# Turning and routing raw tokens tile by tile, gathering the first tokens by channel, and loading the exponential's table ahead

## What is computed

```python
    x = x + mixed @ w_out[i]
    x = x + expert_choice_moe(rms_norm(x, norm2_g[i]), w_router[i], w_gate[i], w_up[i], w_down[i])

def expert_choice_moe(h, w_router, w_gate, w_up, w_down):
    cap = EC_CAPACITY * L // N_EXPERTS                    # 64
    aff = jax.nn.softmax(h.astype(F32) @ w_router.astype(F32), axis=-1)
    gate, idx = lax.top_k(aff.transpose(0, 2, 1), cap)
    xs = jax.vmap(lambda hb, ib: hb[ib])(h, idx)
    a = jnp.einsum('becd,edf->becf', xs, w_gate)
    b = jnp.einsum('becd,edf->becf', xs, w_up)
    y = jnp.einsum('becf,efd->becd', jax.nn.silu(a) * b, w_down)
```

## Time and profile before

| what | before |
|---|---|
| time, median of 3 runs | 2307.78 us (2304.1 to 2308.91) |
| time of the profiled execution | 2311.14 us |
| its span, first to last instruction | 2309.3 us |
| PE busy | 2090.5 us (91% of the span) |
| DVE busy / ACT busy | 698.8 us / 539.4 us |
| large DMAs, share of 16 DMA engines | 53.7% |

### The profile page before, as it was taken

One profiled execution on the slowest core, in us unless ns is written; L12 is line 12 of the kernel. 1 busy time (PEld: TensorE's weight loads), 2 busy tenths in 40 slices (PEclk: granted clock), 3 DMA queues, 4 the chain that ended last, 5 costly groups with the idle time before them and its releaser, 6 DMA issues.

```text
span 2309.3 us, 22263 instructions
## 1 busy us (share of the span) xinstructions
PE 2090.5 (91%) x9138; PEld 1263.4 (55%) x9138; DVE 698.8 (30%) x991; ACT 539.4 (23%) x818; POOL 110.1 (5%) x118
## 2 busy tenths in 40 slices
PE   6999959988989898989898978998999889999998
PEld 5766433323333333333333656787777678887866
DVE  4635130010101010101010667622667333224234
ACT  4224111000000000000000553233433233224134
POOL 2420000000000000000000000230000000000000
PEclk9999979999999999999999988999999989999998
DMA  9410617999999999999999221111113202223320
GB/s 232 143 64 2 255 73 325 427 427 428 428 428 429 428 429 429 428 429 428 428 427 386 108 100 55 37 37 37 55 59 132 83 37 109 83 98 128 105 96 37
DMA packets 46116, 512.28 MB, mean 222 GB/s; under 512 B 5585, under 2 KB 5713, under 8 KB 10593
## 3 DMA queue, kind: packets, MB, share of 16 engines
q1 hardware_dynamic: 43616, 504.72, 53.7%
q0 software_dynamic: 2432, 6.61, 1.3%
HBM read 507.08 MB, written 4.19 MB: 221 GB/s over the span
## 4 chain that ended last, share of the span: by engine, by line
PE 68%; DMA 21%; DVE 7%; ACT 3%; issue 1%; SPq 0%; POOL 0%; ACTq 0%; DVEq 0%
DMA arena<-in_w_gu_dram 19%; PE bank L2127 11%; PE bank L2149 5%; PE bank L852 4%; PE bank L853 4%; PE bank L854 4%; PE bank L536 3%; PE bank L537 3%; PE bank L538 3%; PE bank L2095 3%; PE bank L1996 2%; PE bank L877 2%; PE bank L878 2%; PE bank L879 2%; PE bank L2112 2%; PE bank L1856 1%
## 5 line engine op out<-in xcount | busy, mean ns | idle before, releaser
L2127 PE MATMUL bank<-arena 128*64 128x512 f32 x2048 | 483.7, 629 | 82.4 <-DMA arena<-in_w_gu_dram 81.6
L2127 PEld LDWEIGHTS bank<-arena 128*64 128x64 f32 x2048 | 162.9, 144 | 373.4 <-issue 372.3
L2527 DVE TENSOR_TENSOR arena<-arena,bank 128x256 f32<-128x256 f32 x64 | 27.0, 421 | 691.3 <-ACT arena L2730 691.3
L2149 PE MATMUL bank<-arena 128*64 128x512 f32 x1024 | 232.3, 594 | 0.7 <-ACT arena L2734 0.6
L2730 ACT ACTIVATE arena<-bank 128x256 f32<-128x256 f32 x64 | 24.6, 384 | 561.6 <-PE bank L2127 561.6
L2149 PEld LDWEIGHTS bank<-arena 128*64 128x64 f32 x1024 | 76.4, 137 | 141.1 <-issue 141.1
L852 PE MATMUL bank<-input_rounded,weight_rest 128*128 128x512 f32 x352 | 141.3, 401 | 4.9 <-DVE weight_rest L1274 4.9
L853 PE MATMUL bank<-input_rest,weight_rounded 128*128 128x512 f32 x352 | 141.3, 401 | 0.0
L854 PE MATMUL bank<-input_rounded,weight_rounded 128*128 128x512 f32 x352 | 139.1, 395 | 0.0
L536 PE MATMUL bank<-input_rounded,weight_rest 128*128 128x512 f32 x312 | 133.1, 427 | 4.8 <-DVE weight_rest L927 4.8
L537 PE MATMUL bank<-mix_rest,unit_rounded 128*128 128x512 f32 x312 | 127.5, 409 | 0.0
(11 more groups left out here) (455 smaller groups left out, 2946.9 us busy)
## 6 DMA issues: line engine op xcount, KB each, us to landing
arena<-in_w_gu_dram SPq DMA_DIRECT2D x128, 2048.0 KB, 28.8
arena<-in_w_d_dram SPq DMA_DIRECT2D x64, 2048.0 KB, 25.4
arena<-in_wpack_dram SPq DMA_DIRECT2D x83, 1024.0 KB, 4.9
arena<-in_x_dram SPq DMA_DIRECT2D x2, 2048.0 KB, 8.9
arena<-in_xT_dram SPq DMA_DIRECT2D x2, 1024.0 KB, 6.8
x_kept<-arena SPq DMA_DIRECT2D x4, 512.0 KB, 2.6
arena<-x_kept SPq DMA_DIRECT2D x1, 2048.0 KB, 8.2
out_dram<-arena SPq DMA_DIRECT2D x4, 512.0 KB, 2.6
```

What stands on the lines that cost most here:

```text
L2127: last = mm(ab[64 * x:64 * x + 64, :], xsT[:, k, 64 * x:64 * x + 64], w[x][:, k, :], start=k == 0, stop=k == KD - 1)
L2149: last = mm(bank[4 + n][64 * x:64 * x + 64, :], hidT[c % 2][:, P * t + 64 * x:P * t + 64 * x + 64], w[:, x, t, 512 * n:512 * n + 512], sta ...
```

## The change

Five things are changed.

- The raw tokens are turned in halves of a tile (`turn_half(q)`, q from 0 to 7: tile q % 4, channels of half q // 4) into banks 3, 5 and 7 in turn. ACT copies even q, DVE odd q, to `xturn[q]`, with no gain. The halves are placed among the four groups of half 1 of the output products, and so are the router's products, in halves too (`route_half(q)`), except for what can only be done after the last group.
- The gain `norm2` is multiplied once into `wr` by DVE (128x128, ahead of the first addition of half 1).
- ACT takes a dummy exponential of one column right behind its square root, and all four tiles of `h2` are made after the real exponential (before, one ahead of it and three behind).
- In the choice, the first round reads PSUM (the copy to `w16` is gone). `iota` counts from 1 to 64, so the subtraction of one is gone. The first pair's comparison reads the turned ranks in PSUM, ahead of the copy to `rankc`.
- `first_tokens()` replaces `gather(0)` and `turn_tokens(0)`: 32 products with pieces of `h2` stationary and `ohp` moving (128 columns) give the channel-major tokens at once. The copies to `xtok` for the first pair go.

```diff
@@ PE
             for i in range(NT):
                 mixed_product(1, i, range(KD)).then_inc(S("out1_filled"), 1)
-
-            pe.wait_ge(S("out1_added"), nth("out1_added", 8))
-            for k in range(KD):
-                if k >= 2:
-                    pe.wait_ge(S("h2t_a" if k % 2 == 0 else "h2t_v"), k // 2)
-                for i in range(NT):
-                    last = turn(bank[4 + k % 2][:, P * i:P * i + P], x_res[:, i, P * k:P * k + P], ident)
-                last.then_inc(S("h2_turned"), 1)
...
-            for i in range(NT):
-                for k in range(KD):
-                    last = mm(bank[6][:, NE * i:NE * i + NE], hT[:, k, P * i:P * i + P], wr[:, k, :],
-                              start=k == 0, stop=k == KD - 1)
-            last.then_inc(S("lg_filled"), 1)
+                if i == 0:
+                    turn_half(0)
+                    turn_half(1)
+                if i == 1:
+                    for q in (2, 3, 4):
+                        turn_half(q)
+                if i == 2:
+                    turn_half(5)
+                    route_half(0)
+                    route_half(4)
+                if i == 3:
+                    turn_half(6)
+                    route_half(1)
+                    route_half(5)
+            turn_half(7)
+            route_half(2)
+            route_half(6)
+            route_half(3)
+            route_half(7).then_inc(S("lg_filled"), 1)
...
+            def turn_half(q):
+
+                half, i = q // 4, q % 4
+                pe.wait_ge(S("out1_added"), nth("out1_added", max(q + 1, 4)))
+                if q >= 3:
+                    pe.wait_ge(S("h2t_a" if (q - 3) % 2 == 0 else "h2t_v"), (q - 3) // 2 + 1)
+                for k in range(4):
+                    last = turn(turnbank[q % 3][:, P * k:P * k + P], x_res[:, i, P * (4 * half + k):P * (4 * half + k) + P], ident)
+                last.then_inc(S("h2_turned"), 1)
+
+            def route_half(q):
+
+                half, i = q // 4, q % 4
+                pe.wait_ge(S("h2t_a" if q % 2 == 0 else "h2t_v"), q // 2 + 1)
+                if q == 0:
+                    pe.wait_ge(S("wr_made"), 1)
+                for k in range(4):
+                    last = mm(bank[6][:, NE * i:NE * i + NE], xturn[q][:, k, :], wr[:, 4 * half + k, :],
+                              start=q < 4 and k == 0, stop=q >= 4 and k == 3)
+                return last
@@ PE, first pair
+            def first_tokens():
+
+                pe.wait_ge(S("ohp_made"), 2)
+                for n in range(2):
+                    for k in range(4):
+                        for i in range(NT):
+                            last = mm(bank[(3, 7)[n]][:, P * k:P * k + P], h2[:, i, 512 * n + P * k:512 * n + P * k + P],
+                                      ohp[:, i, :], start=i == 0, stop=i == NT - 1)
+                    last.then_inc(S("xs_turned"), 1)
+                pe.sem_inc(S("xs_filled"), 2)
...
-            gather(0)
-            turn_tokens(0)
+            first_tokens()
@@ DVE
                     tt(out=xs, in0=xs, in1=mixbank[c][i][:, :], op=ALU.add).then_inc(S("out1_added"), 1)
+                    if c == 1:
+                        q = 2 * i + 1
+                        dve.wait_ge(S("h2_turned"), nth("h2_turned", q + 1))
+                        dve.tensor_copy(xturn[q], turnbank[q % 3].rearrange("p (k t) -> p k t", t=P)).then_inc(S("h2t_v"), 1)
...
-            own(dve.tensor_copy(w16, bank[7][0:NE, :]))
...
-            ts(rank[0:NE, :], rank[0:NE, :], -1.0, None, ALU.add).then_inc(S("rank_made"), 1)
             dve.wait_ge(S("rank_turned"), nth("rank_turned", 1))
+            for ab in range(2):
+                tt(out=ohp[:, :, CAP * ab:CAP * ab + CAP], in0=iota.unsqueeze(1).to_broadcast([P, NT, CAP]),
+                   in1=l3[:, :, ab:ab + 1].to_broadcast([P, NT, CAP]), op=ALU.is_equal).then_inc(S("ohp_made"), 1)
             own(dve.tensor_copy(rankc, l3))
@@ ACT
+            turned_half(0)
             for i in range(NT):
+                if i:
+                    turned_half(2 * i)
                 act.wait_ge(S("out1_added"), nth("out1_added", 5 + i))
...
             fn(v2, v2, ACT.Sqrt).then_inc(S("n2sd_made"), 1)
...
+            own(fn(stat[:, 344:345], ones[:, 0:1], ACT.Exp))
...
-            fn(h2[:, 0, :], x_res[:, 0, :], ACT.Copy, scale=r2[:, 0:1]).then_inc(S("h2_first"), 1)
...
             fn(lg, lg, ACT.Exp).then_inc(S("lg_exp"), 1)
-            for i in range(1, NT):
+            for i in range(NT):
                 fn(h2[:, i, :], x_res[:, i, :], ACT.Copy, scale=r2[:, i:i + 1]).then_inc(S("h2_made"), 1)
```

More of the change, by code:

```diff
@@ L274, in program @@
         sqd = view(R0 + 8064, D)
+        xturn = [view(R0 + 512 * q, 4, P) for q in range(8)]
+        turnbank = [bank[3], bank[5], bank[7]]
         def unit_slot(u):
@@ L2083, in _ @@
             last.then_inc(S("rank_turned"), 1)
-            pe.wait_ge(S("h2_made"), nth("h2_made", NT - 1))
+            pe.wait_ge(S("h2_made"), nth("h2_made", NT))
             pe.sem_inc(S("hid_turned"), 2)
@@ L2446, in _ @@
             for c in range(N_OUT1 // 2):
+                if c == 1:
+                    dve.wait_ge(S("wr_in"), 32)
+                    n2 = COLS["norm2"]
+                    tt(out=wr, in0=wr, in1=cols[:, n2:n2 + KD].unsqueeze(2).to_broadcast([P, KD, NE]), op=ALU.mult)\
+                        .then_inc(S("wr_made"), 1)
                 for i in range(NT):
@@ L2459, in _ @@
             dve.wait_ge(S("r2_made"), nth("r2_made", 1))
-            for k in range(1, KD, 2):
-                dve.wait_ge(S("h2_turned"), nth("h2_turned", k + 1))
-                ts(hT[:, k, :], bank[5][:, :], col("norm2", k), None, ALU.mult).then_inc(S("h2t_v"), 1)
             rmx = stat[:, 244:248]
@@ L2481, in _ @@
             top = stat[0:NE, 248:256]
-            own(dve.tensor_copy(w16, bank[7][0:NE, :]))
-            own.wait()
-            for _ in range(CAP // 8):
-                own(dve.max(out=top, in_=w16))
+            for n in range(CAP // 8):
+                left = w16 if n else bank[7][0:NE, :]
+                own(dve.max(out=top, in_=left))
                 own.wait()
-                own(dve.match_replace(out=w16, in_to_replace=top, in_values=w16, imm_value=-1.0))
+                own(dve.match_replace(out=w16, in_to_replace=top, in_values=left, imm_value=-1.0))
                 own.wait()
@@ L2494, in _ @@
             own.wait()
-            own(tt(out=rank[0:NE, :], in0=rank[0:NE, :], in1=sel[0:NE, :], op=ALU.mult))
-            own.wait()
-            ts(rank[0:NE, :], rank[0:NE, :], -1.0, None, ALU.add).then_inc(S("rank_made"), 1)
+            tt(out=rank[0:NE, :], in0=rank[0:NE, :], in1=sel[0:NE, :], op=ALU.mult).then_inc(S("rank_made"), 1)
             dve.wait_ge(S("rank_turned"), nth("rank_turned", 1))
+            for ab in range(2):
+                tt(out=ohp[:, :, CAP * ab:CAP * ab + CAP], in0=iota.unsqueeze(1).to_broadcast([P, NT, CAP]),
+                   in1=l3[:, :, ab:ab + 1].to_broadcast([P, NT, CAP]), op=ALU.is_equal).then_inc(S("ohp_made"), 1)
             own(dve.tensor_copy(rankc, l3))
             own.wait()
-            dve.wait_ge(S("wr_in"), 32)
             dve.sem_inc(S("h_made"), 2)
@@ L2552, in pair @@
                 dve.tensor_copy(ysb[:, 512:1024], bank[5][:, :]).then_inc(S("y_copied"), 1)
-            choose(0)
-            tokens(0)
+            dve.sem_inc(S("xs_copied"), 1)
             turned_tokens(0)
@@ L2697, in _, with turned_half @@
             v2 = stat[:, 236:240]
+            def turned_half(q):
+                act.wait_ge(S("h2_turned"), nth("h2_turned", q + 1))
+                fn(xturn[q], turnbank[q % 3].rearrange("p (k t) -> p k t", t=P), ACT.Copy).then_inc(S("h2t_a"), 1)
+            turned_half(0)
             for i in range(NT):
+                if i:
+                    turned_half(2 * i)
                 act.wait_ge(S("out1_added"), nth("out1_added", 5 + i))
@@ L2704, in _ @@
             fn(v2, v2, ACT.Sqrt).then_inc(S("n2sd_made"), 1)
-            for k in range(0, KD, 2):
-                act.wait_ge(S("h2_turned"), nth("h2_turned", k + 1))
-                fn(hT[:, k, :], bank[4][:, :], ACT.Copy, scale=col("norm2", k)).then_inc(S("h2t_a"), 1)
+            own(fn(stat[:, 344:345], ones[:, 0:1], ACT.Exp))
             act.wait_ge(S("r2_made"), nth("r2_made", 1))
-            act.wait_ge(S("lg_filled"), nth("lg_filled", 1))
             r2 = stat[:, 240:244]
-            fn(h2[:, 0, :], x_res[:, 0, :], ACT.Copy, scale=r2[:, 0:1]).then_inc(S("h2_first"), 1)
             act.wait_ge(S("lg_made"), nth("lg_made", 1))
             fn(lg, lg, ACT.Exp).then_inc(S("lg_exp"), 1)
-            for i in range(1, NT):
+            for i in range(NT):
                 fn(h2[:, i, :], x_res[:, i, :], ACT.Copy, scale=r2[:, i:i + 1]).then_inc(S("h2_made"), 1)
@@ L2750, in pair @@
                 fn(ysb[:, 0:512], bank[4][:, :], ACT.Copy).then_inc(S("y_copied"), 1)
-            tokens(0)
```

(3 more changed lines are left out.)

5 lines of the change are left out of this document (1 added, 4 removed).

## The result

| | before | after |
|---|---|---|
| median of 5 runs | 2307.78 us | 2294.41 us |
| lowest, highest | 2304.1, 2309.39 | 2294.09, 2297.61 |
| ratio, 95% interval | | 0.9937, 0.9924 to 0.995 |
| profiled execution, its span | 2311.14, 2309.3 | 2294.12, 2292.3 |

The forecast was 2298.8 us, 9.0 faster, with a range from 2294.5. The gain is 13.4 us, and the median lies 0.1 us under the range.

A forecast was written before the change was run, and what follows sets the result against it. The MoE's full DMA weight stream, begun by the first `gate_up`, was taken as the bound. Gains of 3.7 + 1.7 + 1.65 + 1.9 = 9.0 us from the median of 2307.8 gave 2298.8 us; 8-in-10 range 2294.5 to 2304.5.

The forecast's parts named there:

- What bounds the kernel: MoE weight stream: DMA full at 428 GB/s, so bringing the first `gate_up` forward brings the whole stream and second block forward.
- They hold 64 records of turns and 64 of narrow products: Count for the 18.69 us from half 1's last addition to the router's end: 128 records, 14.1 us at 0.11 each.
- The term of turning and routing: Last addition of half 1 to the router's products: gain 4.6 us at full clock, 3.7 after the clock's cost.
- The clock in the tail: Last 32 records behind the last wide group: cost between nothing and 3.1 us if the clock falls, taken as 0.9.
- The exponential: Logits to DVE going on: table load moved ahead and copy to `h2` moved behind, gain 1.7 us.
- the choice: Copy to `w16` gone 0.7, subtraction gone 0.45, comparison earlier 0.5: together 1.65 us.
- First tokens: Start of first tokens to first `gate_up`: 10.2 us in place of 12.08, gain 1.9, with 4.45 us at the lower clock.
- PE did not wait for copies: Rival, turns: one copy of 0.7 us in the open at each of eight halves, gain 3.4, 2304.4 us; chance 0.05.
- The weight loads were hidden: Slower rival: stationary pieces of 128 columns loaded in the open, 247 ns each, 26 us lost, 2325 us; chance 0.03.
- That rival's 192 records: Records of 128 stationary columns said to pay an open load: 128 in turning and routing, 64 in first tokens.
- The clock did not stay down in the first tokens: Rival: clock stays at 0.50 through first tokens, 14.6 us in place of 10.2, gain 2.4, 2305.4 us; chance 0.08.
- The rival in which it falls soon behind the wide products: All 64 records behind the last wide group at 0.21 us, 5.5 more than in the sum, 2304.3 us; chance 0.04.

The follow-up runs named there:

- the eight: Eight profiled executions, of the changed kernel and variants sharing its tail; the 32 last narrow records took 3.64 us in four, 5.66 to 5.83 in the others.
- the paced products: Changed kernel plus products on PE whose results nothing reads, placed behind DVE's rounds during the choice: 2290.87 us, ratio 0.9928; with the last wide group also cut, 2291.08 us.
- the kernel with everything behind: Changed kernel with all turns and narrow products behind the last wide group: 2302.15 us, ratio 0.9977.
- 13 in a row: Changed kernel plus 13 products of 512 columns on PE, results unread, while it waits for the choice: 2294.16 us, ratio 0.994.

## Why the prediction was wrong, step by step

**What bounds the kernel** was right. The first `gate_up` came 13.30 us earlier, the refill 13.31, the stream's last wait ended 13.25 earlier; 12.94 of it come from the change and 0.36 from ahead of it, where nothing was changed.

**The step that failed: "They hold 64 records of turns and 64 of narrow products".** The term of turning and routing was mis-sized by a count. I had carried the rule that a product is two records in float32 over to the turns, and read the row with 8 turn records as one channel group, where it is two groups of four. A turn is one record of 0.109 us. So PE's work is 96 records, not 128: 3.5 us less. 18.69 - 96 x 0.11 is 8.1, and 8.15 was measured. Turning everything twice put those 32 records in, and 3.5 us with them. One look at the groups by line and form of the kernel before, 298.7 to 317.6 us, would have shown it:

```profile
L2073 PE MATMUL bank<-arena 128*128 128x16 f32 x64 | 10.8, 322 | 0.9 <-ACT arena L2707 0.9
L2066 PE MATMUL bank<-arena 128*128 128x128 f32 x32 | 4.6, 283 | 2.5 <-ACT arena L2707 1.7 <-DVE arena L2451 0.8
```

**The clock in the tail**, for which I took off 0.9, cost nothing in this execution, 2.0 in another, and 1.0 on average over the eight. Mechanism and bounds were right, and as an average so was the size: that it was nothing in the profiled execution is chance. There the 3.5 and the 0.9 are the whole of the miss in this term. With the count right and the rest as it stands, the forecast would have been 2295.3 us, inside the range; the last 0.9 us to 2294.41 lie within the scatter of the runs. Nor had I said what in the gain comes from the clock. The place of the records keeps it up, which was in the number, since I priced all at 0.11; with all of them behind the wide groups it is lost again.

**The exponential** (1.7, measured 1.68) and **the choice** (1.65, measured 1.65) were right. The Trainium skill (ScalarE: Activation LUTs, What ACT_TABLE_LOAD costs) has a drain of about 1.4 us beside the load; the rows did not show it, and neither did the runs: undoing the early load cost 1.27 us, not 2.7.

**First tokens** gave 1.46 in place of 1.9: the clock rose at 332.8 us, 5.1 us behind their start, not 4.45 (0.50 to 332.0, then 0.59 over the next microsecond). The mechanism held: in each execution without the paced products the clock rose during these 64 records, which took 8.83 to 10.32 us.

**The rivals.** PE did not wait for copies. The weight loads were hidden: 32 narrow records, each with a load of 128 stationary columns, took 3.64 us in the tail. (That rival's 192 records hold the same wrong count; there are 160.) The clock did not stay down in the first tokens. The rival in which it falls soon behind the wide products did not happen in the profiled execution. A milder form of it did in four of the eight with this tail: the clock fell among the last 32 records and cost some 2 us, not 5.5. In the kernel with everything behind it fell at 303.5 us. For a fall in the tail at all, the chance of 0.04 was too low. What the Trainium skill says of transposes (TensorE: Matmul & The Clock Gate, Part 4: PE-mode transpose), that they don't count as busy for the clock, is not decided by these runs: in that kernel turns and narrow products stood mixed, and in the kernel before the clock was still 1.00 when the turns had ended and the narrow products began.

The range was too narrow, since its lower end was built on a term whose count I had not checked. That the median fell only 0.1 us outside it says little for the forecast: the mis-sized term alone was 3.5 us off.

## What to carry to other kernels

Count the records of each kind by line before pricing them: a matmul and a transpose of the same shape need not be the same number of records. Small products are best placed between wide ones, where they cost their own time alone; in a row of their own they also lost the clock here, in some 70 of 96 records. If PE must wait some 15 us for a chain on another engine and then has a burst of work on the critical path, products paced by that chain can keep the clock up for it (2.4 us of 9.8 or 1.9 of 9.3 here). With 13 in a row and then 2.9 us in which PE ran only four small records, the clock was lost again. And where executions differ by microseconds ahead of the edit, compare the stretch between two marks of the program, not only the times.

## What the runs showed of the hardware

The clock's falls and rises are not tied to the program. In the changed kernel's tail it held 1.00 to the end of the 32 last narrow records in one execution; in another it fell when about a third of them had run (0.61 over 302.5 to 308.2 us), and they took 3.64 and 5.67 us. That is a scatter of 2 us from one place, a good part of the runs' own scatter (3.5 us, 2294.09 to 2297.61). A transpose of 128x128 float32 is one record of 0.109 us at the upper level, while a product with 128 moving columns is two of about 0.11. The table's load took 1.28 us and the exponential began 0.01 us behind it.
